# A two-block transformer on one core: programs without loops, the first four modulation units on TensorE, hosted units spread over the tiles

## What is computed

```
cond = jax.nn.silu(c)
mod = (cond @ ada_w[layer] + ada_b[layer])[:, None, :]
shift_m, scale_m, gate_m, shift_f, scale_f, gate_f = jnp.split(mod, 6, axis=-1)
h = rmsnorm(x, norm_mix_g[layer]) * (1.0 + scale_m) + shift_m
...
x = x + gate_m * mixed
h = rmsnorm(x, norm_ffn_g[layer]) * (1.0 + scale_f) + shift_f
x = x + gate_f * swiglu(h, ffn_w_in[layer], ffn_w_out[layer])
```

## Time and profile before

| | |
|---|---|
| median of 3 runs | 2947.21 us (2944.55 to 2950.08) |
| the profiled execution: span of the core | 2947.8 us, 40274 instructions |
| mean granted TensorE clock | 0.929 |
| PE busy | 2595.9 us, 88% |
| DVE busy | 1953.4 us, 66% |
| ACT busy | 1067.9 us, 36% |
| DMA | 407.12 MB, mean 138 GB/s |
| first weight matmul starts | 60.87 us |
| attention starts | 143.67 us |

### The profile page before, as it was taken

The page is one execution under the profiler, slowest core; times in us unless marked ns, Lnnn a source line. Parts: engine busy times, 40 slices in busy tenths (PEclk is TensorE's granted clock), DMA queues, the critical chain, the costliest instruction groups (busy, mean ns, idle before and its releaser), DMA issues.

```text
span 2947.8 us, 40274 instructions
## 1 busy us (share of the span) xinstructions
PE 2595.9 (88%) x14718; PEld 2213.9 (75%) x14718; DVE 1953.4 (66%) x3172; ACT 1067.9 (36%) x1563; POOL 55.3 (2%) x56
## 2 busy tenths in 40 slices
PE   3988899866788869999977998999989999888998
PEld 3857898845788858888855566888868888775998
DVE  7857987845477778888854657888363333665655
ACT  3464335442243353222232434222242222434544
POOL 1010000001100000000000000000000000000000
PEclk7968999978899979999988999999999999899999
DMA  7906995520057746666530214666233332331563
GB/s 262 324 1 196 307 300 151 148 63 1 1 158 207 205 131 175 188 191 185 165 91 17 63 59 127 185 187 185 88 109 95 95 99 83 98 92 32 158 189 116
DMA packets 618346, 407.12 MB, mean 138 GB/s; under 512 B 27767, under 2 KB 555862, under 8 KB 618070
## 3 DMA queue, kind: packets, MB, share of 16 engines
q1 hardware_dynamic: 618198, 405.19, 47.6%
HBM read 404.09 MB, written 1.05 MB: 137 GB/s over the span
## 4 chain that ended last, share of the span: by engine, by line
PE 69%; DVE 18%; ACT 4%; DMA 4%; issue 4%; DVEq 0%; SPq 0%; POOL 0%; ACTq 0%
PE ps L1451 58%; DVE ada_acc L1737 5%; DMA ada_raw<-in_ada_w 4%; DVE w_lo L1710 2%; PE ps L1463 1%; DVE tmp L1946 1%; PE ps L1220 1%; DVE h_lo L1940 1%; PE ps L1197 1%; PE ps L758 1%; PE ps L756 1%; DVE y_conv L1837 1%; PE ps L748 1%; PE ps L1209 1%; ACT w_hi L1623 1%
## 5 line engine op out<-in xcount | busy, mean ns | idle before, releaser
L1451 PE MATMUL ps<-h_hi,w_hi 128*128 128x256 f32 (+1 forms) x3048 | 1023.6, 336 | 76.4 <-DVE h_lo L1940 56.6
L1623 ACT CAST w_hi<-raw 128x1024 fp32r<-128x1024 f32 (+3 forms) x557 | 555.1, 997 | 1300.7 <-PE ps L1451 1217.6
L1451 PE MATMUL ps<-h_hi,w_lo 128*128 128x256 f32 (+1 forms) x3048 | 1008.0, 331 | 0.0
L1451 PE MATMUL ps<-h_lo,w_hi 128*128 128x256 f32 (+1 forms) x3048 | 1007.7, 331 | 0.0
L1710 DVE TENSOR_TENSOR w_lo<-raw,w_hi 128x1024 fp32r<-128x1024 f32 (+3 forms) x557 | 643.8, 1156 | 209.9 <-ACT w_hi L1623 205.2
L1451 PEld LDWEIGHTS ps<-h_hi,w_hi 128*128 128x128 f32 x3048 | 589.9, 194 | 155.8 <-issue 79.8
L1451 PEld LDWEIGHTS ps<-h_lo,w_hi 128*128 128x128 f32 x3048 | 590.8, 194 | 50.2
L1451 PEld LDWEIGHTS ps<-h_hi,w_lo 128*128 128x128 f32 x3048 | 591.9, 194 | 47.1
L1737 DVE SCALAR_TENSOR_TENSOR ada_acc<-ada_raw,cond,ada_acc 128x512 f32<-128x512 f32 x644 | 460.7, 748 | 24.2 <-DMA ada_raw<-in_ada_w 15.5
L1451 PE MATMUL ps<-a_hi,w_hi 128*128 128x256 f32 (+1 forms) x1056 | 360.5, 341 | 6.1 <-DVE a_lo L1798 6.1
L1451 PE MATMUL ps<-a_hi,w_lo 128*128 128x256 f32 (+1 forms) x1056 | 357.8, 339 | 0.0
(11 more groups left out here) (298 smaller groups left out, 1978.5 us busy)
## 6 DMA issues: line engine op xcount, KB each, us to landing
raw<-in_ffn_w_in SPq DMA_DIRECT2D x264, 512.0 KB, 4.7
ada_raw<-in_w_mod SPq DMA_DIRECT2D x144, 512.0 KB, 4.0
raw<-in_ffn_w_out SPq DMA_DIRECT2D x96, 512.0 KB, 5.1
ada_raw<-in_ada_w SPq DMA_DIRECT2D x80, 512.0 KB, 4.6
raw<-in_ffn_w_out SPq DMA_DIRECT2D x48, 384.0 KB, 3.5
raw<-in_gdn_w_in SPq DMA_DIRECT2D x33, 512.0 KB, 4.1
raw<-in_w_in SPq DMA_DIRECT2D x26, 512.0 KB, 3.9
raw<-in_attn_w_in SPq DMA_DIRECT2D x24, 512.0 KB, 5.7
```

The lines of the kernel that those rows point to most:

```text
L1451: last = mm(ps[0:m, slot, 0:n], w[:, slot, k * P:k * P + m], v[:, s0 + k, 0:n], start=(k == 0 and w is w_hi and v is hi), stop=(k == lin.k ...
L1623: nc.scalar.copy(w_hi[:, slot, 0:n], raw[:, slot, 0:n]).then_inc(s_hi, 1)
```

## The change

Five things are changed; the plan of stages and the units that each hosts are the same.

1. All programs are written out, with no hardware loop and no register arithmetic.
2. The first four units move from DVE to PE. The silu of the condition stands in column 0 of a stationary block of 32 columns (`cond_wide`, the other conditions in columns 1 and 2, the rest zero), and the rows come as eight DMAs of 1 MB (128 rows x 2048 columns, a ring of four). 32 matmuls of 32x512 (fp32) write four groups of 32 PSUM partitions of one bank; ACT copies the bank, PE turns it in four transposes, DVE copies 16 columns. The vector DMAs are issued by ACT instead of SP.
3. The tables are loaded after the load of tile 8; the angles are made on DVE at tile 10 and turned into sine and cosine on ACT at tile 14. The ACT and DVE splits of the first four tiles move into the first norm.
4. A hosted unit's pairs are spread over the tiles by `pair_at`; in a stage of 16 tiles and four units pairs 0 and 1 of the first unit are at tile 0, pair 2 at tile 1, pair 3 at tile 2, then one pair at each tile, and the last tile has none. `unit_sums` stands on PE right after the tile of pair 3 (tiles 2, 6, 10, 14; in a stage of 8 tiles and two units 2 and 6; in one of 8 and one unit 5), `ada_sum` on DVE in the next tile, ahead of the epilogue. Nothing is carried over.
5. One PSUM address in the delta recurrence (`second_values`) moves within its banks.

```
-FIRST = 8
+FIRST = 4
...
+    def unit_tiles(self, u):
+
+        return [(self.n - 1) * (u + i) // self.ada[2] for i in range(2)]
+
+    def pair_at(self, u, k):
+
+        a, b = self.unit_tiles(u)
+        return a + k * (b - a) // (KD // 2)
...
+            def first_rows(k):
+
+                if k >= FIRST:
+                    sp.wait_ge(event("first_rows_multiplied"), k - FIRST + 1)
+                src = dram["ada_w"][0][k * P:(k + 1) * P, 0:FIRST_UNITS * HALF]
+                sp.dma_start(ada_first[:, k % FIRST], src).then_inc(s_first[k % FIRST], 16)
...
+                if g == 8:
+                    load_tables()
+                for host, u, k in after_tile.get(g, ()):
+                    unit_pair(host, u, k)
...
+                    for p, (u, k) in enumerate(pairs):
+                        g = st.g0 + (st.pair_at(*pairs[p - 2]) + 6 if p >= 2 else st.pair_at(u, k) + 4)
+                        after_tile.setdefault(g, []).append((st, u, k))
...
+            def first_products(k):
+
+                pe.wait_ge(s_first[k % FIRST], 16 * (k // FIRST + 1))
+                for j in range(FIRST_UNITS):
+                    last = mm(ps[32 * j:32 * j + 32, ADA_A, :], cond_wide[:, k, :], ada_first[:, k % FIRST, j * HALF:(j + 1) * HALF],
+                              start=(k == 0), stop=(k == KD - 1))
+                last.then_inc(event("first_rows_multiplied"), 1)
...
+                for j in range(lin.n):
+                    tile(lin, j, w if j == 0 else None)
+                    for u in lin.sums(j):
+                        unit_sums(lin, u)
...
+                    act.wait_ge(event("first_rows_multiplied"), KD)
+                    nc.scalar.copy(ada_acc[:, 0], ps[:, ADA_A, :]).then_inc(event("first_sums_copied"), 1)
...
+                    if a0["n"] == 0:
+                        for g in range(2):
+                            split(*tile_of(g))
...
+                    for j in range(st.n):
+                        nxt = tile_of(st.g0 + j + AHEAD)
+                        if nxt:
+                            split(*nxt)
+                        for u in st.sums(j - 1):
+                            ada_sum(st, u)
+                        for u, k in st.pairs(j):
+                            ada_rows(st, u, k)
+                        if st.g0 + j == 10:
+                            angles()
+                        epilogue(st, j)
```

More of the change, by code:

```diff
@@ L250, in number @@
             s.silu0, s.sq0, s.ssq0 = silus, sqs, ssqs
-            s.unit0 = units
+            s.unit0, s.row_unit0 = units, rows
             s.conv0 = conv
@@ L500, in units_before @@
         def units_before(st):
[L501 to L517, removed]
-            return stages[i - 1] if isinstance(stages[i - 1], Linear) and carries(stages[i - 1]) else None
+            i = next(n for n, s in enumerate(stages) if s is st)
+            done_ = [s for s in stages[:i] if isinstance(s, Linear) and s.ada]
+            count = sum(s.ada[2] for s in done_)
+            for s in stages[:i]:
+                if not isinstance(s, Linear) and s[0] == "modulation":
+                    count += s[3]
+            return count
         def blk(j, n=1):
@@ new lines, in _ @@
+            ahead = set()
+            for i, st in enumerate(stages):
+                if isinstance(st, Linear):
+                    for j in range(st.n):
+                        if st.g0 + j not in ahead:
+                            load(st, j)
+                elif st[0] == "modulation":
+                    for k in range(2):
+                        first_rows(k)
+                    sp.dma_start(x_in[:], dram["x"][0].rearrange("(t p) d -> p t d", p=P)).then_inc(s_xin, 16)
+                    sp.dma_start(ctx_in[:], dram["ctx_2"][0].rearrange("(t p) d -> p t d", p=P)).then_inc(s_xin, 16)
+                    for k in range(2, KD):
+                        first_rows(k)
+                elif st[0] in ("attention", "delta"):
+                    for j in range(RING):
+                        load(stages[i + 1], j)
+                        ahead.add(stages[i + 1].g0 + j)
@@ new lines, in _ @@
+                    for j in range(st.n):
+                        nxt = tile_of(st.g0 + j + AHEAD)
+                        if nxt:
+                            split(*nxt)
+                        for u in st.sums(j - 1):
[4 more added lines that the diff above has]
+                            angles()
+                        epilogue(st, j)
+                        if squared and j:
+                            squares(st, j - 1)
@@ L1951, in _ @@
                         lo(len(parts) - 1)
+                        if a0["n"] == 0:
+                            for g in range(1, AHEAD):
+                                split(*tile_of(g))
                     elif mode == "replace":
```

409 lines of the change are left out of this document (145 added, 264 removed).

## The result

The changed kernel takes 2996.98 us (median of 4, 2994.63 to 3001.94) against 2948.07 us of the kernel before beside it: ratio 1.0165, 95% interval 1.0151 to 1.018. It is 49 us slower, where I forecast 9 us faster.

What follows compares the result with a forecast made beforehand. PE was taken as the bound, busy 2595.9 of 2947.8 us, so only its idle time could be won. Start and project -10.2, loops -10.5 and the hosted-stage and attention terms summed to -9.3: 2938 us, range 2926 to 2951.

Steps and rivals of the forecast that it cites:

- the spread of the hosted units: Hosted stages: same DVE work, but PE asks for sums right behind the last pair and waits wherever DVE lags; terms per stage.
- Two dual units, stages 157 and 181: Stages with 256 tokens, bound by DVE: the second sum, once carried into the next stage, now stands behind tile 6; +4 together.
- Stages 32 to 72: Single-unit stages paced by DMA and two row buffers: a sum can no longer hide in the next stage; +4.5 us together.
- Stage 133: One dual unit: PE's 4.67 us wait behind its fifth tile shrinks, since DVE has kept up but for 1 us; -3.6.
- Stages 209 and 315: Stages starting behind a norm: PE waits 3.3 us for a sum where it waited none; +3.4 each, +6.8 together.
- 225, 249, 331, 355: Residual stages with 512 tokens and two units: the same wait with PE tiles of 5.6; +1.6 each, +6.4 together.
- The start: Before the first weight matmul: DVE's work on four units goes, the rows' loading sets the time; matmul at 40.5, -20.4 us.
- The project stage: It inherits work from the start: tables +4, angles +2.5, colder ring +0.8, last unit's sum +2.9; +10.2 us, bounds 3 and 14.
- Rival 4: In delta_in straight code is no better than the loop, which keeps 3.85 a tile: 2948.5; chance 0.05.
- rival 1: In the start the new products' column groups run one after another: first weight matmul at 53.2, 2951; chance 0.15.
- Rival 2: Stages hold back more: project stage at +14 and the spread at its upper bounds, 2952, at half 2945; chance 0.22.
- Rival 3: In hosted stages the earlier asking for sums costs nothing, as DVE makes up its lag: 2921 to 2925; chance 0.15.

Runs made afterwards that it cites:

- e1: The changed kernel with pairs, sums and row DMAs of the hosted units back at their old places: 2932.64 us, 0.9945 of before.
- e4: The changed kernel with every unit's pairs at tiles 0, 0, 1, 2 and its sum on PE behind the fourth tile: 2949.1 us, 0.9999 of before.
- e10: The changed kernel with four buffers for the modulation rows instead of two, without added issue delays behind attention and mixer: 2983.56 us, 1.0112 of before.
- e5: e1 with PE's turns of vector tiles 1 to 3 moved behind the seventh row block's products: 2925.08 us, 0.9918 of before.
- e9: e5 with the 2.2 MB of tables transferred a second time behind the first: 2928.91 us, 0.9932 of before.
- e7: e6 with the 1.4 MB of tables that attention doesn't use loaded during attention: 2917.92 us, 0.9892 of before.
- e6: e5 with positions and frequency column loaded, and the angles and sines made, in the start: 2920.69 us, 0.9904 of before.
- e2: The kernel before with its loops written out and nothing else changed: 2940.86 us, 0.9967 of before.

## Why the prediction was wrong

The sign failed on one step, **the spread of the hosted units**. In the sum it cost 15.6 us (12.7 behind attention and 2.9 in the project stage); e1 shows 64. "PE waits wherever DVE lags" was right, the sizes that I gave it were not. I priced each sum by how much later DVE would be than PE at that place, but in stages where DVE paces I let the work that PE no longer does ahead cost 2 us, while it costs the two tiles themselves, 5.4.

- *Two dual units, stages 157 and 181* (with 165 and 189): +2 each in the sum, measured +6.3 each. The stages themselves grew by 12.5 and 12.7, and the next ones gave 6.2 and 6.6 back.
- *Stages 32 to 72*: +4.5 forecast, bounds 1 to 8; measured +23.2, and 2.4 back in 80 and 92. I named two buffers and 4.6 us of landing and then did not work out that the first unit's four pairs within three tiles need the third and fourth row in less time than that; e4 and e10 show it for half of the loss.
- *Stage 133*: -3.6 forecast, measured +0.7. The step that failed was "with pairs at tiles 0, 1, 3, 5 DVE has kept up but for 1 us". The sum stands later than before here (behind tile 5, not 4) but directly behind its last pair, and PE waited 4.20 us:

```profile
844.59 1.97 PE L1422 MATMUL ps<-consts,ada_acc 128*128 128x128 f32 x8 [4.20 <-DVE ada_acc L1662]
```

  e4, whose pairs stand at tiles 0, 0, 1, 2 and whose sum stands behind tile 3, waits 1.51 us and makes the stage 4.2 us shorter than before. So a tile between the last pair and the sum counts for more here than a late place.
- *Stages 209 and 315*: +3.4 each forecast, +5.6 measured. The sum waited nearly as computed, 3.3 us by the text, and in the trace

```profile
1149.54 1.69 PE L1422 MATMUL ps<-consts,ada_acc 128*128 128x128 f32 x8 [2.90 <-DVE ada_acc L1662]
```

  The mechanism is right, the size was off. The tile with wait and turn took 9.85 us in 209, where one with a turn alone takes 6.2: 3.6 more. The tile behind it took 6.67 at a granted clock of 0.82, where 5.6 is the rule: 1.1 more. And the fourth unit's turn, 0.9 us, now stands in the stage itself and not in the next one. I had counted only the first of the three.
- *225, 249, 331, 355*: +6.4 forecast, +10.8 measured. The first sum waits 2.05 us in 225 and 331 and 1.37 in 249 and 355; in 225 the tile behind it took 7.21 us instead of 5.7, at a granted clock of 0.77.
- *The start*: -20.4 forecast, -13.5 measured. The step that failed was that the products "fit between 11.6, when the condition is ready, and 30": I read the condition's turn and overlooked that the turns of the other vectors stand between it and the first product. With that undone (e5) it is -20.4.
- *The project stage*: +10.2 (8.9 with attention's -1.3), bounds 3 and 14; measured +21.7, and attention started at 152.2 us, not at 133. 7 of it is the spread (e1), for which the sum had 2.9. The other 14.7 stand against +4 for the tables, +2.5 for the angles and +0.8 for the ring. The tables cost by what queues behind them: in the changed kernel rows issued at 66.3 landed at 79.3, and DVE waited 5.15 us for them. A second transfer adds 5.7 (e9), taking 1.4 of the 2.2 MB away gives 3.5 (e7), moving the angles 4.7 (e6). e7 is still 5.4 above before; the 0.79 MB that it keeps are a part of that, for the rest no run gives the cause.
- *Loops*: -10.5 forecast, -12.8 measured for their group in the changed kernel and -10.0 for the loops alone (e2). Right. Rival 4 is out. The moved PSUM address has no run of its own; it stands in this group, where e2 leaves 1.4 us for it and all else.
- *Column groups*: side by side, as forecast; rival 1's mechanism did not happen. I had misread the window 616 to 620 of the earlier trace rows: of its nine instructions two have 16 columns, and a full one takes 0.43 us back to back (L722 at 619.46, the next at 619.88), not 0.40. Four 32-column products also take 0.43, a factor of 4. The Trainium skill's 2.38 for three tiles ("TensorE: Matmul & The Clock Gate", Part 3) was the careful value, and the weight loads, whose overlap I had doubted, held nothing up.
- *Rival 2* was the right kind, at a quarter of its size: I bounded its parts one by one at 8, 8 and 8 and added only a few microseconds of each.
- *Rival 3* was added up wrongly: 4.5, 4, 6.8 and 6.4 are 21.7, not 17, which gives 2916 us. And the parts of "same" give 0.33, not 0.30. Neither bears on the outcome.

The forecast differs by 62 us from the spans' +52.4. In order: stages 32 to 92 16 us, project with attention 13, 157 to 189 9, start 7, 133 5, the 512-token stages 9, others 3.

## What to carry to other kernels

In a queue in program order a small dependent step (here four transposes) should stand behind as much other work as its user allows: where the producer sets the pace, moving it two tiles forward cost the two tiles (stage 157), and where it stands directly behind the producer's last part it waits even if it stands late (stage 133). Spreading the producer's work evenly helps only if a tile is left between its last part and the consumer. Two buffers with a landing time of 4.6 us held up four uses in three tiles of 2.9 us. A large transfer costs by what queues behind it, so it belongs where nothing urgent follows. The sound way to judge such a change is to ask at each such wait how many tiles the waiting engine has behind it when the last input comes, before and after.

## What the runs showed of the hardware

- Four fp32 products with 32 stationary columns each, on different groups of 32 PSUM partitions, took 0.114 us an instruction of 512 columns in a chain of 32, against 0.43 for a full one back to back. The weight loads between them held nothing up: a group of four starts every 0.43 us.
- The hardware loop cost DVE 0.64 us a tile of five instructions in delta_in (and e2 with all tiles straight), 10 us in all (e2); in the other stages it cost nothing that a stage's length shows.
- Rows issued behind a transfer of 2176.5 KB landed after 13.0 us (issued at 66.3 us in the changed kernel), where the median is 4.6.
- A wait of PE of 5 to 9 us was dearer than itself, before and after the change: the next tile of 24 matmuls took 4.0 to 5.3 us instead of 2.7 to 3.0, at a mean granted clock of 0.52 to 0.69 (seven such waits in the changed kernel).
